# First experts of a two-block transformer step: 80 blocks in the fixed layout in place of 88

## The reference, cut to what matters

```python
logits = (h @ w_router) + b_router
top_val, top_idx = lax.top_k(logits, 4)
gates = softmax(top_val)
...
u = (xb @ w1[e] + b1[e])                       # w1[e] is 1024 x 2048
glu = minimum(u[:, 0::2], 7.0)
lin = clip(u[:, 1::2], -7.0, 7.0)
act = glu * sigmoid(1.702 * glu) * (lin + 1.0)
y = act @ w2[e] + b2[e]                        # w2[e] is 1024 x 1024
out[token] += y * g
```

## Time and profile before

| | |
|---|---|
| median of 3 runs | 2887.63 us (2875.38 to 2887.97) |
| the profiled execution | 2878.46 us |
| its span, first to last instruction | 2876.7 us |
| TensorE matmuls busy | 2258.6 us, 79% |
| DVE, ACT, POOL busy | 1075.0, 741.5, 118.3 us |
| moved by DMA | 622.97 MB, mean 217 GB/s |
| TensorE's granted clock, mean | 0.88 of full speed |

### The profile page before, as it was taken

The page is one execution under the profiler, slowest core; times in us unless marked ns, Lnnn a source line. Parts: engine busy times, 40 slices in busy tenths (PEclk is TensorE's granted clock), DMA queues, the critical chain, the costliest instruction groups (busy, mean ns, idle before and its releaser), DMA issues. The chain is left out here.

```text
span 2876.7 us, 49673 instructions
## 1 busy us (share of the span) xinstructions
PE 2258.6 (79%) x21092; PEld 1354.3 (47%) x21092; DVE 1075.0 (37%) x1892; ACT 741.5 (26%) x1812; POOL 118.3 (4%) x135
## 2 busy tenths in 40 slices
PE   4978798669999988898889839992996476764880
PEld 2944366534444433333334327892664255554660
DVE  2235554432222322222222252226665655442114
ACT  3223454201111111011111112124665214321231
POOL 0000000000000000000000020000000211000001
PEclk8989889879999999899999969995997688785995
DMA  5256601178899999999999762110000000304973
GB/s 204 102 213 240 253 1 66 61 309 342 365 420 419 420 421 422 422 420 421 422 422 420 309 222 96 59 32 5 1 1 1 1 1 8 125 15 181 417 285 119
DMA packets 146787, 622.97 MB, mean 217 GB/s; under 512 B 33349, under 2 KB 65093, under 8 KB 93321
## 3 DMA queue, kind: packets, MB, share of 16 engines
q1 hardware_dynamic: 117048, 572.35, 49.2%
q0 software_dynamic: 8352, 30.41, 2.9%
q10 hardware_dynamic: 21168, 17.06, 1.9%
HBM read 585.42 MB, written 34.37 MB: 215 GB/s over the span
## 5 line engine op out<-in xcount | busy, mean ns | idle before, releaser
L2023 PE MATMUL psum<-w,x 128*32 128x512 f32 x5696 | 659.2, 612 | 75.9 <-DMA w<-in_w_mlp 64.4
L2023 PEld LDWEIGHTS psum<-w,x 128*32 128x32 f32 x5696 | 182.5, 112 | 492.1 <-issue 378.3
L2032 PE MATMUL psum<-w,act_turned 128*32 128x256 f32 x5696 | 325.8, 381 | 3.8 <-DVE act_turned L2188 3.5
L2179 DVE TENSOR_TENSOR u<-psum,x 128x512 f32<-128x512 f32 x89 | 61.6, 692 | 701.0 <-PE psum L2023 701.0
L731 PE MATMUL psum<-high 128*128 128x512 f32 (+3 forms) x832 | 292.1, 351 | 36.7 <-DVE low L753 36.7
L731 PE MATMUL psum<-high,low 128*128 128x512 f32 (+3 forms) x832 | 291.0, 350 | 0.0
L731 PE MATMUL psum<-low,high 128*128 128x512 f32 (+3 forms) x832 | 291.0, 350 | 0.0
L2032 PEld LDWEIGHTS psum<-w,act_turned 128*32 128x32 f32 x5696 | 187.0, 111 | 168.7 <-issue 63.2
L753 DVE TENSOR_TENSOR low<-weight_slots,high 128x1024 fp32r<-128x1024 f32 (+3 forms) x84 | 89.3, 1066 | 290.1 <-ACT high L747 289.7
L731 PEld LDWEIGHTS psum<-high 128*128 128x128 f32 x832 | 159.5, 192 | 58.0 <-ACT high L747 37.6
L731 PEld LDWEIGHTS psum<-high,low 128*128 128x128 f32 x832 | 159.3, 191 | 20.0
(11 more groups left out here) (460 smaller groups left out, 2764.0 us busy)
## 6 DMA issues: line engine op xcount, KB each, us to landing
w<-in_w_mlp SPq DMA_DIRECT2D x192, 2048.0 KB, 28.3
weight_slots<-in_w_ada SPq DMA_DIRECT2D x12, 2048.0 KB, 11.1
weight_slots<-in_w_mod SPq DMA_DIRECT2D x12, 2048.0 KB, 10.9
weight_slots<-in_w_in SPq DMA_DIRECT2D x9, 2048.0 KB, 8.3
gu<-in_w_gate SPq DMA_DIRECT2D x16, 1024.0 KB, 11.8
gu<-in_w_up SPq DMA_DIRECT2D x16, 1024.0 KB, 14.6
down<-in_w_down SPq DMA_DIRECT2D x16, 1024.0 KB, 19.5
weight_slots<-in_w_out SPq DMA_DIRECT2D x6, 2048.0 KB, 10.7
```

Of the source, the lines that this page charges most:

```text
L2023: mm = pe.matmul(psum[g * RB:(g + 1) * RB, bank, :], b.turned[:, kc, q * RB:(q + 1) * RB], w[:, i, g * BANK:(g + 1) * BANK], start=kc == 0 ...
L2032: mm = pe.matmul(psum[g * RB:(g + 1) * RB, 2 + parity, 0:YW], b.act_turned[:, parity, kc, :], w[:, i, g * YW:(g + 1) * YW], start=kc == 0, ...
L2179: step.reach(dve.tensor_tensor(b.u[:], psum[:, bank, :], b.bias[:], ALU.add), s.biased, at + 1)
```

## The change

One line. It gives 80 fixed blocks in place of 88, over the same 31 turns: rank 1 has 4 in place of 5, ranks 15 to 17 have 2 in place of 3, ranks 27 to 30 have 1 in place of 2. The tiles of the fixed part become 20 in place of 22. The loop is as it was.

```diff
-BY_RANK1 = [6, 5, 4, 4, 4] + [3] * 13 + [2] * 13 + [0]
+BY_RANK1 = [6] + [4] * 4 + [3] * 10 + [2] * 12 + [1] * 4 + [0]
```

## The result

| | before | after |
|---|---|---|
| median of 6 runs | 2882.53 us (2875.38 to 2887.97) | 2864.86 us (2858.33 to 2869.61) |
| the profiled execution | 2878.46 us | 2859.98 us |
| its span | 2876.7 us | 2858.2 us |
| TensorE matmuls busy | 2258.6 us | 2191.6 us |
| moved by DMA | 622.97 MB | 620.73 MB |

The ratio is 0.994, with a 95% interval from 0.9924 to 0.9956: 17.7 us faster by the medians, 12.7 to 21.9 us by the interval. A later control of the same kernel, beside 24 runs of the kernel before, gave 0.995 (0.993 to 0.9971), 14.5 us by the medians. The forecast was 15 us and 2868 us, with a range from 2853 to 2885 us.

What follows compares the result with a forecast made beforehand. The prediction took moving 32 experts' weights by DMA, at 421 GB/s, to bound the first experts' stage. Traffic 6.4, second gap 8.5 and end 0 summed to 15 us saved, giving 2868 us, range 2853 to 2885.

Steps and rivals of the forecast that it cites:

- The balance by turn: First experts' stage: two turns with five blocks need 63 us of DMA traffic but only 52 us of TensorE.
- TensorE's work worth nothing by itself: First experts' stage: the 83 us TensorE loses count only where DMA engines idled for a free slot, plus traffic removed.
- (a): First experts' stage: gathers and stores of two tiles and code for eight blocks go, worth 6.4 us, bounds 5 to 7.
- (b): Early turns of the stage: the DMA engines' second gap, at 731 to 741 us, closes; worth 8.5 us, bounds 0 to 9.
- the rule of 31 us against 35: Ring of 11 slots: a four-block turn frees a slot after 31 us, within 35 us of queued transfers, so no gap.
- Rival 1: The second gap moves to a four-block turn instead of closing; gain only 6.4 us, 2877 us; chance 0.14.
- (c): End of the stage's loading, where the DMA share drops: taken as no gain, 0 us, with 6 us as the other end.
- (d): After the last weights land: nothing changes, the overflow block runs as before, 1641.82 to 1661.87 us in the old profile.
- Waits on weights: TensorE in the stage: its waits for weight loads grow from 64 us to some 130 us.
- rival 4: Stage slower: waits lower TensorE's clock, which bounds below a mean of 0.82; at 0.75, 73 us slower, 2955; chance 0.04.
- the issue expected near 720 us: Turn 2: the weight load that ended the second gap, issued at 739.96 us before, would be issued at 718 to 721.
- The fifth rival: Loop after the fixed blocks: a rank overflows and forces a second pass, 35 us slower, given as 2903 us; chance 0.03.

Runs made afterwards that it cites:

- Two kernels with 80 and 88 blocks: 80: the run with the gap kept, 0.9976; 88: changed kernel with eight blocks added back at ranks late in the stage, second gap closed, 0.9971 to before.
- A TensorE relieved of 208 us: Changed kernel whose fixed blocks multiply only two of eight k-steps of w2; 0.9937 to the kernel before, way to the pass 1024.8 us.
- the ring of 9: Changed kernel with a ring of 9 weight slots in place of 11; 1.0059 to the kernel before, 1073.4 us from the stage's first issue to the loop's pass.
- the run with the gap kept: Changed kernel's 80 blocks, but turns 1 and 2 keep 2 and 5 blocks and other ranks give up blocks instead; 0.9976 to the kernel before.
- the two passes: Changed kernel, still 80 blocks, but the second-fullest expert gets 3 in place of 4, so the loop makes two passes; 1.0052 to the kernel before.

## Why the prediction was right

**The balance by turn, and TensorE's work worth nothing by itself: shown.** Two kernels with 80 and 88 blocks have ratios of 0.9976 and 0.9971, which noise cannot tell apart, though TensorE works 56 us less in one of them. A TensorE relieved of 208 us shortened the way to the pass by 11 us.

**(a) Traffic, 6.4 us: right.** 6.1 us on the way to the pass, 6.9 us by the ratio, 7.2 us by the packets. The packets bear out the terms: 3.2 us for ACT's queue (forecast 3.1), 2.6 for POOL's (2.7), 0.6 for code (0.6); the rest is weight loads whose packets took 0.8 us less in all.

**(b) The second gap, 8.5 us: right in size, by a step with a wrong number.** Measured were 7.8 us on the way to the pass, 8.4 us by the ratio, and 9.1 us of the engines' idle time. The step said that the load behind the gap would be issued at 718 to 721 us, with 10 us to spare. It was issued at 730.08 us (728.6 us in the control):

```profile
700.47 3.60 PE L2023 MATMUL psum<-w,x 128*32 128x512 f32 x16 [4.30 <-DMA w<-in_w_mlp]
703.88 3.64 PE L2032 MATMUL psum<-w,act_turned 128*32 128x256 f32 x64
...
727.99 4.46 PE L2023 MATMUL psum<-w,x 128*32 128x512 f32 x40
```

I had put the blocks of turn 2 where they stood before. But turn 2 now starts before its weights are there, and its first product waits for them in pieces, until 700.47 us. All later blocks of the turn, and the release of the slot, move with it. What saved the term is that the rule of 31 us against 35 counts from the fourth load's landing, and the queue moves with that as well: from 700.4 us the issue came 29.6 us later, and the seventh queued load landed at 736.5 us, 36.0 us later. The margin was 6 us (5 us in the control), not 10. Rival 1 had named just this delay; the ring of 9 shows what happens when the margin is gone.

**(c) The end, 0 us: about right, with the sign the other way.** The share before the pass stood at 0.46 over 14 us. The engines' idle time in the last 40 us before the pass is 5.7 to 6.4 us in the profiles of before, 7.8 and 7.1 us in those of the changed kernel, so the end did not close but lost about 1 us more. With another 1 us in the stretch before it, this takes the 7.2 and 9.1 us by the packets down to the 14.0 us of the way.

**(d) Past the landing: right on the mean, with a scatter that I had left out.** From the pass's first product to the first gather of the combining, the three profiles of before took 20.7, 22.1 and 23.2 us, the changed kernel 21.3 and 22.6, the run with the gap kept 25.0. The second product of the pass takes 3.66 us at the full clock, 5.35 us where the clock rises in its midst, and 6.54 us in the 25.0 us run.

**Waits on weights, 130 us forecast: 103 us measured.** Of the 83 us, 60 show as less busy time. The other 23 are an estimate of what more time at the low clock took back (631 ns on the mean in place of 612), so less was left to be waited away: 39 us on weights and 10 us before the pass. The mean over the stage, 0.93, stayed far above the 0.82 at which rival 4 begins.

**The total.** The sum gave 15 us; the stage gave 14.0 us in the control, the medians 17.7 and 14.5 us. The surplus of the first pair of medians over the stage is within the scatter of the rest; part of it may be the few us behind the stage that the runs neither show nor exclude. That 15 and 14.0 us lie so close is in part luck: (a) and (b) came out 0.8 and 0.6 us larger by the packets, and the 2 us lost elsewhere were in no term.

**Signs and slips.** The stage ended at 1652.5 us in the first profile, not near 1649, and the issue expected near 720 us came at 730. The fifth rival's 2903 us is a slip: 35 us slower than the kernel before would be 2918, on the base that the other rivals use.

## What to carry to other kernels

Where TensorE and the DMA engines are both full, ask what each piece of work removed would have let start earlier; here eight of 88 blocks, 83 us of TensorE, were worth 14 us, of which some 8 came from the layout of two turns, in one of the two places where the ring ran dry. A ring's reach can be checked turn by turn with one inequality, the time until the next slot comes free against the transfers still queued. And when an edit is small against the scatter of the whole, measure it between two marks inside the profile: three profiles of the kernel before agreed to 1 us over 1050 us of the stage (two of the changed kernel only to 3 us), and differed by 8 us over what lay behind it.

## What the runs showed of the hardware that was not expected

**Code is fetched by the same DMA engines.** In the stage 91 packets of 16 KB were code, one for about every block. Before the last landing of most profiles, the DMA share falls from full to about a half and stays there for some 8 to 11 us, in the profiles of before with a short break. That is what it would look like if half of the engines carried something that the others do not, and so fell behind while all were busy. The length of the tail fits this. After some 700 us without a pause (the ring of 9, whose last gap ended at 949 us) it was 6 us at 0.51; before the second of the two passes, with seven transfers that kept the engines busy for some 30 us, there was next to none, with 1.04 from 1660 to 1672 us and 0.19 over the last 2 us. Whether the something is the code stays open. Six microseconds more than its gap explains came off the way to the pass when the code packets fell from 83 to 53, but only 2.0 of them are the packets' own time, and the profile does not name the engine of a packet.

**The low clock after a long wait costs at the end, too.** The pass follows an idle time of 8 to 9 us before the change and of 18 to 20 us in the changed kernel, its control and the run with the gap kept, and from its start to the first gather takes 20.7 to 25.0 us. In the last 2 us before the pass the granted clock was at its low level, 0.50, in every profile. So the first product begins there (8.4 to 9.9 us in place of 7.05); what varies is how far into the pass the clock stays low. In the 25.0 us run it was 0.76 over the first product and the wait behind it and 0.65 over the rest; in the profile after, 0.84 and 1.00. The longer idle time did not by itself make the pass longer: 20.7 to 23.2 us before, 21.3 and 22.6 after. The Trainium skill (TensorE: Matmul & The Clock Gate, section HAM oscillation) tells that a wait for a transfer leaves the matmuls behind it cold; these rows agree, and the middle of the stage shows its limit, a mean granted clock of 0.94 although each pair of turns waits.
